# Two-layer streaming encoder trunk: head additions moved to VectorE, reload DMAs moved to GpSimd's queue, layer 0 put in another order

## The chip, the cores and the metric

One core of one Trainium2 chip runs the whole kernel. The metric is the device time of one execution in microseconds; the median of 3 runs of the kernel before is 2255.37 us (2248.55 to 2256.2). Engines: TensorE (PE; its weight loads are PEld), VectorE (DVE), ScalarE (ACT), GpSimd (POOL), SyncE (SP). A DMA is issued from the queue of SP, ACT or POOL.

## The reference

1088 frames (1024 of a new stream, 64 of a running one) of 1024 channels pass two layers:

```python
hn = rmsnorm(x, g_mix); proj = hn @ w_in           # u_a | u_b, 512 channels each
# A: 32 groups x 64 complex diagonal states
lam_bar = exp(lam * dt); b_bar = ((lam_bar - 1) / lam) * b
h[t] = lam_bar * h[t-1] + b_bar @ u_a[t]; y = Re(c @ h) + d * u_a
z = gelu(y); y_a = z * sigmoid(z @ w_glu)
# B: mean over the last 2/4/8/16 frames minus the frame, per group of 128 channels
y_b = ((window_sum / count - u_b) @ w_pool) * pool_scale
x = x + concat([y_a, y_b]) @ w_out
x = x + square(relu(rmsnorm(x, g_ffn) @ w_ff1)) @ w_ff2
```

Then a last RMSNorm. The final states and the last 15 rows of u_b are outputs too. All is float32.

## The kernel before

Channels lie on partitions, frames on the free axis: x is [128, 8, 1088]. Frames are ordered so that a block of 8 successive frames is one column of J = 136 (T = 8 * 136). A product in float32 precision is three float32r passes, high x high, low x high and high x low (`products`, L427): each weight block (512 KB in `w_raw`, two buffers) is split on ScalarE (`split_hi`, L649) and VectorE (`split_lo`, L874), and so are the activations (`h_high`/`h_low`, L879). A tile of a product is 128 x 1088 in one of two PSUM buffers; for 8 k-blocks it takes TensorE 12 us, for 4 some 6 us. `tile_done` counts tiles of TensorE, `tile_free` those that VectorE has read out. Two small PSUM buffers serve all little matmuls, in the order of `small_numbers`. Each engine's order is written out by hand; an engine does its instructions strictly in that order.

**Head.** ACT's queue loads x; ScalarE and VectorE square it by turns, GpSimd adds the squares up (`add_squares`, L1378), and h_high, h_low of all eight rows are made. `angles`, `discretised` and `rotations` on VectorE, `exponents` and `sines` on ScalarE make layer 0's tables (powers of lambda, rotations over 136 blocks by doubling: piece 0 to length 16, piece 1 to 64, pieces 2 and 3 the last step for each half).

**Window tiles (t = 0 to 7).** u_a tiles (`win_a`) go to DRAM and come back as blocks (`turn_u`); u_b tiles (`win_b`) go into `ub`, which lies in x's place. Between tiles TensorE does `turns` (transposes of the drive weights), `drives` (block inputs to states) and `kernels` (the kernel inside a block). VectorE makes `drive_weights`, `carry_weights`, `fix_kernel`, the window sums (`pooled`), and turns the states back (`pre`), scans them (`scan`) and turns them on (`post`), in quarters q = 0 to 3.

**Second half of the mixer.** Four pool tiles, `y_b` on VectorE; eight tiles `wob(n)` (half of w_out) that VectorE adds to x, which has to be loaded again first (L394, L399: SP's queue, behind `carry_weights` and eight DMAs of `intra_weights`, L390, in pieces of 512 B). `carry(q)` on TensorE makes y of quarter q from intra and carry weights; ScalarE (`carried`) empties the small buffers and stores to DRAM, SP loads `y_a` (L403, after block B_GLU + 1 has been asked for, which needs the low half of block B_WOB + 3, made in VectorE's `wob(3)`). `gelus` and z_high on ScalarE, z_low on VectorE, then the gate product, the other half of w_out, and the feed-forward part in 8 chunks (cc) of 4 up-tiles (m = 0 to 3) and 8 down-tiles. In layer 0 these chunks also hold layer 1's tables. x overlaps the pool buffers, `y_a` the states, z_high the rotations, and `kst` (stage for the intra kernel) the buffer `work_s`.

Of the kernel before, what the change touches and what calls it, by code (L numbers as in the profile page):

```python
# [9 lines left out]
ALU = mybir.AluOpType  # L10
ACT = mybir.ActivationFunctionType

P = 128
# [3 lines left out]
BLK = 8  # L17
# [4 lines left out]
KD = DM // P  # L22
# [37 lines left out]

def small_numbers():
# [16 lines left out]
    for t in range(2, 8):  # L78
        if 3 <= t < 7:
            drives(0, t - 3)  # L80
        if t < 6:
            turns(0, t - 2)
        if t >= 4:
            kernels(0, t - 4)
# [12 lines left out]
def hybrid_trunk(nc, x_in, w_blocks, w_pool, prep_in, gain0, layer_in, dstate_in,  # L97
# [10 lines left out]
    with ExitStack() as ctx:  # L108
# [50 lines left out]
        class Prep:  # L159


            def __init__(self, l):
# [15 lines left out]
                if l == 0:  # L178
                    z = E
                    self.rot_tmp = at("rot_products_0", o, [P, 2, 512])  # L180
# [56 lines left out]
        first_sq = sem("first_sq")  # L237
# [7 lines left out]
        pp_in = sem("pp_in")  # L245
        dd_in = sem("dd_in")
# [78 lines left out]
        PREP_CHUNKS = {cc: cc - 1 for cc in range(1, 5)}  # L325
# [4 lines left out]
        def _(sp):  # L330
# [28 lines left out]
            def load_prep(l):  # L359
                sp.dma_start(prep_of[l].pp[:, :], prep_in[l, :, 0:C_HIST]).then_inc(pp_in, 16)  # L360
                sp.dma_start(dd[:, :], dstate_in[l]).then_inc(dd_in, 16)

            sp.dma_start(g0[:, :], gain0).then_inc(const_in, 16)
            fetch(0)
            load_prep(0)
            fetch(1)
            for l in range(LAYERS):
                LB, LT = l * NB, l * NT
                for b in range(2, B_FF + 2):
# [12 lines left out]
                    if b == B_WOB + 2:  # L382
                        sp.wait_ge(tile_done, LT + KD)
                        sp.wait_ge(cy_out, 128 * (l + 1))
                        sp.dma_start(cy[:, :, :, :], cy_dram[l]).then_inc(cy_in, 16)
                        sp.wait_ge(k_out, 128 * (l + 1))
                        sp.wait_ge(k_zero, 32)
                        for tau in range(BLK):
                            a = CH * (BLK - 1 - tau)
                            sp.dma_start(kin[CH * tau:CH * tau + CH, :, :],  # L390
                                         k_dram[l, :, :, a:a + P]).then_inc(kin_in, 16)
                        sp.wait_ge(tile_free, LT + T_POOL + KA + 2)
                        for m in range(6):
                            sp.dma_start(x[:, m, :], (x_in, x_hist)[l][m]).then_inc(x_back[m], 16)  # L394
                    if b == B_WOB + 3:
                        sp.wait_ge(hist_out_s, 16 * (l + 1))
                        sp.wait_ge(fin_out, 16 * (l + 1))
                        for m in range(6, KD):
                            sp.dma_start(x[:, m, :], (x_in, x_hist)[l][m]).then_inc(x_back[m], 16)  # L399
# [5 lines left out]
                for b in range(B_FF + 2, NB + 2):  # L405
# [6 lines left out]
                    if l == 0 and b == B_FF + 8 * 6:  # L412
# [8 lines left out]
        def _(pe):  # L421
# [27 lines left out]
            def sum_part(phase, c):  # L449
                a, b = CHUNKS[c]  # L450
                out = small_at(SM["sum", phase, c])
                pe.wait_ge(sq_added, 7 * phase + 7)
# [48 lines left out]
            for l in range(LAYERS):  # L501
                LB, LT = l * NB, l * NT

                for t in range(KD):
# [12 lines left out]
                    if l == 0:  # L517
# [4 lines left out]
                        if t >= 4:  # L522
                            kernels(0, t - 4)
# [51 lines left out]
                if l == 0:  # L575
                    for n in range(4):
                        wob(n)
                    carry(0)
                    carry(1)
                    wob(4)  # L580
                    carry(2)
                    wob(5)
# [3 lines left out]
                else:  # L586
                    wob(0)
                    carry(0)
                    wob(1)
# [54 lines left out]
        def _(act):  # L644
# [12 lines left out]
            def finish(m, phase, gain, keep):  # L657

                if m > 2:
                    act.wait_ge(sq_added, 7 * phase + m - 2)  # L660
# [60 lines left out]
            for m in range(KD):  # L721
                act.dma_start(x[:, m, :], x_in[m]).then_inc(x_in_s[m], 16)
            split_hi(0)
            act.wait_ge(const_in, 16)
            for m in range(KD):
                act.wait_ge(x_in_s[m], 16)
                if m % 2 == 0:
                    if m > 2:
                        act.wait_ge(sq_added, m - 2)
                    act.activation((tr if m else rms)[:, :], x[:, m, :], ACT.Square).then_inc(sq_made, 1)  # L730
                act.activation(hhi[:, m, :], x[:, m, :], ACT.Copy, scale=g0[:, m:m + 1]).then_inc(hhi_made, 1)
                if m == 1:
                    exponents(0)
                if m == 3:
                    sines(0)
            split_hi(1)
            act.wait_ge(ones_set, 1)

            for l in range(LAYERS):
                LB, LT = l * NB, l * NT  # L740
                for t in range(KD):
# [3 lines left out]
                    if l == 0:  # L745
# [4 lines left out]
                        if t >= 4:  # L750
                            kernels(0, t - 4)
# [29 lines left out]
                def gelus(q):  # L781
                    act.wait_ge(ya_in[q], 16 * (l + 1))
                    act.activation(ya[:, q, :], ya[:, q, :], ACT.Gelu_apprx_tanh).then_inc(gelu_made, 1)
                    act.wait_ge(gelu_made, l * KA + q + 1)
                    if q == 0:
                        act.wait_ge(st_v, l * 4 + 4)
                    act.activation(zhi[:, q, :], ya[:, q, :], ACT.Copy).then_inc(z_made, 1)

                if l == 0:
                    wob_ahead(0)  # L790
                    wob_ahead(1)
                    carried(0)
                    carried(1)
                    carried(2)
                    wob_ahead(2)
                    carried(3)
                else:
                    carried(0)
                    wob_ahead(0)
                    carried(1)  # L800
                    wob_ahead(1)
                    carried(2)
                    carried(3)
                    wob_ahead(2)
                for q in range(4):
                    gelus(q)
# [53 lines left out]
        def _(v):  # L860
# [20 lines left out]

            def inverse(phase):
# [35 lines left out]
            def discretised(l):  # L918
# [3 lines left out]
                v.wait_ge(prep_a, l * 4 + 4)  # L922
                tt(d.th[:, :, :], d.k[:, :, :], d.k[:, :, :], ALU.mult)
# [42 lines left out]
            def doubled(l, n, h):  # L966
# [549 lines left out]
```

## Time and profile before

| | |
|---|---|
| profiled execution | 2253.69 us, span 2251.9 us, mean granted clock 0.973 |
| PE / PEld busy | 2106.2 / 2061.9 us (94% / 92%) |
| DVE / ACT / POOL busy | 1120.2 / 421.3 / 120.3 us |
| TensorE waits over the span, by releaser | h_low 36.3; x 27.5; x_quarter 12.0; y_b_low 8.8; issue (intra weights, layer 1) 7.9 |
| DMA landing, median from issue | w_raw 512 KB 3.6 us; y_a 544 KB 4.3; cy_dram 256 KB (POOL) 2.9; bt_dram 512 KB (POOL) 5.7; prep_in 736 KB 9.8 in the head |

A row of the timeline reads: start us, duration us, engine, line, operation, output<-inputs, count, and in brackets the idle time of that engine just before and what ended it. Rows of successive instructions of one kind are merged (xN). TensorE has 146 us of idle time in the span, 82 of them before 300 us.

### The profile page before, as it was taken

What the parts mean: (1) busy time and instruction counts of PE and PEld (TensorE: products, weight loads), DVE (VectorE), ACT (ScalarE), POOL (GpSimd) and SP (SyncE); (2) the same over time, 40 slices, a digit from 0 to 9 for tenths busy, and PEclk for the clock granted to TensorE, in tenths of its full rate; (3) what the DMA queues carried; (4) which work ended last, traced back from release to release, by engine and by line L of the source; (5) the groups of instructions that cost most, each with busy time, mean ns of one, the idle gap of its engine ahead of it and who ended that gap; (6) DMA issues with size and microseconds to landing.
All of it is one profiled execution on the core that took longest, in us unless ns stands there. A gap on an engine that the chain in (4) does not pass through costs nothing. (4 is left out here: it accounts for less than half of the span.)

```text
span 2251.9 us, 29009 instructions
## 1 busy us (share of the span) xinstructions
PE 2106.2 (94%) x12894; PEld 2061.9 (92%) x12894; DVE 1120.2 (50%) x1622; ACT 421.3 (19%) x483; POOL 120.3 (5%) x80
## 2 busy tenths in 40 slices
PE   4796799899999999999999989999999999999995
PEld 3785799899999999999999879999999999999995
DVE  8896646836344453434356843552433334333344
ACT  3121143201111111111131114420110111111021
POOL 4000003000000000000030000300000000000002
PEclk7898999999999999999999999999999999999997
DMA  3325521112111111311134382111111111111111
GB/s 143 103 64 96 171 58 52 47 38 96 48 57 58 54 54 49 121 48 47 38 117 133 78 174 69 38 47 48 47 38 47 47 38 47 47 47 38 48 38 79
DMA packets 72060, 152.63 MB, mean 68 GB/s; under 512 B 7392, under 2 KB 32512, under 8 KB 71296
## 3 DMA queue, kind: packets, MB, share of 16 engines
q1 hardware_dynamic: 56240, 123.25, 18.3%
q10 hardware_dynamic: 12960, 17.96, 2.5%
q0 software_dynamic: 2736, 9.57, 1.2%
q8 instruction: 101, 1.65, 0.3%
q14 instruction: 23, 0.19, 0.0%
HBM read 123.23 MB, written 27.53 MB: 67 GB/s over the span
## 5 line engine op out<-in xcount | busy, mean ns | idle before, releaser
L1214 DVE TENSOR_TENSOR x<-tile,x 128x816 f32<-128x816 f32 x320 | 216.4, 718 | 519.8 <-PE tile L427 491.7
L427 PE MATMUL tile<-h_high,w_high 128*128 128x408 f32 (+1 forms) x1920 | 432.0, 333 | 41.8 <-DVE h_low L879 36.3
L427 PE MATMUL tile<-h_low,w_high 128*128 128x408 f32 (+1 forms) x1920 | 426.0, 330 | 0.0
L427 PE MATMUL tile<-h_high,w_low 128*128 128x408 f32 (+1 forms) x1920 | 425.9, 330 | 0.0
L427 PEld LDWEIGHTS tile<-h_high,w_high 128*128 128x128 f32 x1920 | 324.0, 190 | 49.7 <-DVE h_low L879 26.7
L427 PE MATMUL tile<-hidden_high,w_high 128*128 128x408 f32 (+1 forms) x1536 | 341.6, 331 | 11.3 <-DVE x L1214 6.2
L427 PE MATMUL tile<-hidden_low,w_high 128*128 128x408 f32 (+1 forms) x1536 | 338.9, 329 | 0.0
L427 PE MATMUL tile<-hidden_high,w_low 128*128 128x408 f32 (+1 forms) x1536 | 338.8, 329 | 0.0
L649 ACT ACTIVATE w_high<-w_raw 128x1024 fp32r<-128x1024 f32 x164 | 172.4, 1051 | 824.2 <-PE tile L427 807.9
L427 PEld LDWEIGHTS tile<-h_low,w_high 128*128 128x128 f32 x1920 | 323.2, 190 | 1.2
L427 PEld LDWEIGHTS tile<-h_high,w_low 128*128 128x128 f32 x1920 | 323.1, 190 | 1.2
L1330 DVE SCALAR_TENSOR_TENSOR work_r<-tile,rms 128x816 f32<-128x816 f32 (+1 forms) x128 | 86.7, 719 | 377.6 <-PE tile L427 377.4
L427 PEld LDWEIGHTS tile<-hidden_high,w_high 128*128 128x128 f32 x1536 | 257.0, 189 | 18.1 <-issue 12.7
L874 DVE TENSOR_TENSOR w_low<-w_raw,w_high 128x1024 fp32r<-128x1024 f32 x164 | 210.4, 1283 | 101.3 <-ACT w_high L649 101.3
L427 PEld LDWEIGHTS tile<-hidden_low,w_high 128*128 128x128 f32 x1536 | 256.7, 189 | 0.9
L427 PEld LDWEIGHTS tile<-hidden_high,w_low 128*128 128x128 f32 x1536 | 256.7, 189 | 0.8
L829 ACT ACTIVATE hidden_high<-work_r 128x1088 fp32r<-128x1088 f32 x64 | 71.4, 1116 | 647.2 <-DVE work_r L1330 647.2
L1378 POOL TENSOR_TENSOR rms<-rms,work_s 128x1088 f32<-128x1088 f32 x20 | 54.6, 2732 | 1214.3 <-ACT work_s L662 1189.5
L1333 DVE TENSOR_TENSOR work_s<-work_r 128x1088 f32<-128x1088 f32 x64 | 82.7, 1292 | 2.2
L1338 DVE TENSOR_TENSOR hidden_low<-work_s,hidden_high 128x1088 fp32r<-128x1088 f32 x64 | 82.2, 1284 | 0.0
L427 PE MATMUL tile<-y_b_high,w_high 128*128 128x408 f32 (+1 forms) x192 | 44.2, 339 | 20.7 <-DVE x L1214 20.2
L879 DVE SCALAR_TENSOR_TENSOR h_low<-x,layer_params,h_high 128x1088 fp32r<-128x1088 f32 x24 | 43.9, 1830 | 27.3 <-ACT h_high L664 27.3
(156 smaller groups left out, 1445.2 us busy)
## 6 DMA issues: line engine op xcount, KB each, us to landing
w_raw<-w_blocks SPq DMA_DIRECT2D x164, 512.0 KB, 3.6
x<-x_t ACTq DMA_DIRECT2D x8, 544.0 KB, 12.4
u_blocks<-ua_dram SPq DMA_DIRECT2D x64, 68.0 KB, 2.7
x<-x_t SPq DMA_DIRECT2D x8, 544.0 KB, 13.7
ya_dram<-u_blocks ACTq DMA_DIRECT2D x64, 68.0 KB, 2.2
y_a<-ya_dram SPq DMA_DIRECT2D x8, 544.0 KB, 4.3
x_kept<-x ACTq DMA_DIRECT2D x8, 544.0 KB, 2.7
x<-x_kept SPq DMA_DIRECT2D x8, 544.0 KB, 13.0
```

The costliest lines, as they stand in the source:

```text
L427: mm = pe.matmul(ps[tile][:, c, 0:(b - a) * J], lhs, xt[:, k, a * J:b * J], start=(first and n == 0), stop=(last and n == 2))
L649: act.activation(whi[:, b % 2, :], raw[:, b % 2, :], ACT.Copy).then_inc(whi_made, 1)
L829: act.activation(ghi[:, m, :], tr[:, :], ACT.Square).then_inc(ghi_made, 1)
L874: v.tensor_tensor(wlo[:, b % 2, :], raw[:, b % 2, :], f32(whi[:, b % 2, :]), ALU.subtract).then_inc(wlo_made, 1)
L879: v.scalar_tensor_tensor(hlo[:, m, :], x[:, m, :], gain[:, m:m + 1], f32(hhi[:, m, :]), ALU.mult, ALU.subtract).then_inc(h_made, 1)
L1214: ins = v.tensor_tensor(xt, pt_, xt, ALU.add)
L1330: ins = v.scalar_tensor_tensor(out, pt_, 0.0, r, ALU.max, ALU.mult)
L1333: v.tensor_tensor(ts[:, :], tr[:, :], tr[:, :], ALU.mult).then_inc(sq_v, 1)
L1338: v.tensor_tensor(glo[:, m, :], ts[:, :], f32(ghi[:, m, :]), ALU.subtract).then_inc(hid_made, 1)
L1378: pool.tensor_tensor(rms[:, :], rms[:, :], (tr, ts)[m % 2][:, :], ALU.add).then_inc(sq_added, 1)
```

## The change

- Head: `add_first` on VectorE adds the squares (semaphore `first_added`), ScalarE squares all eight rows. `exponents(0)` and `angles(0)` go first, `sines(0)` after h_high of row 0, `discretised(0)` after the eight rows. The parameters come in two DMAs (160 KB ahead of the first weight block).
- The reloads of x, `carry_weights` and `intra_weights` go from SP's queue to POOL's, in layer 0 with six rows of x ahead of the intra weights.
- Layer 0: VectorE's rotation pieces, `pre`, `scan`, `post` and `fix_kernel` in another order; `kernels` after tiles 3, 4, 6, 7; TensorE's `wob` and `carry` in another order, in layer 1 `wob(1)` ahead of `carry(0)`.
- `gelus(0)` stands before `carried(2)`; the others alternate with z_high.
- Layer 1's tables over chunks 0 to 5 of layer 0's feed-forward part.

```diff
+KERNEL_AFTER = {3: 0, 4: 1, 6: 2, 7: 3}
-        PREP_CHUNKS = {cc: cc - 1 for cc in range(1, 5)}
+        PREP_CHUNKS = {cc: cc - 2 for cc in range(2, 6)}
# SP
             sp.dma_start(g0[:, :], gain0).then_inc(const_in, 16)
+            sp.dma_start(prep_of[0].pp[:, 0:C_BRE], prep_in[0, :, 0:C_BRE]).then_inc(pp_in, 16)
             fetch(0)
-            load_prep(0)
+            load_more(0)
             fetch(1)
-                    if b == B_WOB + 2:
-                        (carry_weights, intra_weights x8, x rows 0 to 5)
-                    if b == B_WOB + 3:
-                        (x rows 6 and 7)
# TensorE, layer 0 / layer 1
-  wob(0..3) carry(0) carry(1) wob(4) carry(2) wob(5) carry(3) wob(6) wob(7)
+  wob(0) wob(1) wob(2) carry(0) wob(3) wob(4) carry(1) wob(5) carry(2) carry(3) wob(6) wob(7)
-  wob(0) carry(0) wob(1) carry(1) wob(2) ...
+  wob(0) wob(1) carry(0) carry(1) wob(2) ...
# ScalarE, head
+            exponents(0)
             split_hi(0)
             for m in range(KD):
                 act.wait_ge(x_in_s[m], 16)
-                if m % 2 == 0:
-                    ...
                 act.activation(hhi[:, m, :], x[:, m, :], ACT.Copy, scale=g0[:, m:m + 1])
+                if m == 0:
+                    sines(0)
+                if m > 2:
+                    act.wait_ge(first_added, m - 2)
+                act.activation(((tr, ts)[m % 2] if m else rms)[:, :], x[:, m, :], ACT.Square)
# ScalarE, carries: layer 0 / layer 1
+  wob_ahead(0) carried(0) wob_ahead(1) carried(1) gelus(0) wob_ahead(2) carried(2) carried(3)
+  wob_ahead(0) carried(0) carried(1) wob_ahead(1) gelus(0) carried(2) carried(3) wob_ahead(2)
+                act.wait_ge(st_v, l * 4 + 4)
+  gelus(1) z(0) gelus(2) z(1) gelus(3) z(2) z(3)
# VectorE, head
+            def add_first(m):
+                v.wait_ge(sq_made, m + 1)
+                if m > 1:
+                    v.wait_ge(first_added, m - 1)
+                v.tensor_tensor(rms[:, :], rms[:, :], (tr, ts)[m % 2][:, :], ALU.add).then_inc(first_added, 1)
+            angles(0)
             split_lo(0)
             for m in range(KD):
                 v.wait_ge(x_in_s[m], 16)
                 low_h(m, m, g0)
+                if m > 1:
+                    add_first(m - 1)
+            add_first(KD - 1)
             split_lo(1)
+            discretised(0)
# VectorE, layer 0
+  inverse(0) win_a(0) rotations(0, 0) win_a(1) rotations(0, 1) drive_weights(0, 0) win_a(2)
+  drive_weights(0, 1) carry_weights(0, 0) win_a(3) drive_weights(0, 2) carry_weights(0, 1)
+  fix_kernel(0, 0) win_b(4) rotations(0, 2) drive_weights(0, 3) win_b(5) carry_weights(0, 2)
+  fix_kernel(0, 1) pooled(0, 3) win_b(6) carry_weights(0, 3) pooled(0, 2) fix_kernel(0, 2)
+  win_b(7) pooled(0, 1) fix_kernel(0, 3) pooled(0, 0) y_b(0..3)
+  pre(0, 0, late) scan(0, 0) wob(0) post(0, 0) wob(1) pre(0, 1, late) scan(0, 1) wob(2)
+  post(0, 1) rotations(0, 3, late) wob(3) pre(0, 2, late) wob(4) scan(0, 2) post(0, 2)
+  wob(5) pre(0, 3, late) scan(0, 3) post(0, 3) wob(6) wob(7)
# VectorE, feed-forward of layer 0: after up-tile m of chunk cc
-  cc 0: angles, discretised, rotations 0, rotations 1; cc 1, m 0: rotations 2 and 3
-  cc 1 to 4: drive_weights at m 1, carry_weights at m 3
+  cc 0: angles, discretised, rotations 0 (m 0 to 2); cc 1: rotations 1, 2, 3 (m 0 to 2)
+  cc 2 to 5: drive_weights at m 1, carry_weights at m 2
# GpSimd
-            add_squares(0)
+                carry_weights_out(0, q); kernels_out(0, q)      # q = 0 to 3
+            carry_in(0)          # waits tile_done, cy_out
+            x_first_back(0)      # waits tile_free of y_b(3), then rows 0 to 5
+            kernels_in(0)        # waits k_out, k_zero, then 8 DMAs
+            states_out(0)        # waits st_v
+            x_last_back(0)       # waits the stores, then rows 6 and 7
             add_squares(1)
             ...
+            carry_in(1); kernels_in(1); x_first_back(1); states_out(1); x_last_back(1)
```

## Rows read from the trace of the kernel before

**Rows 1.** The page, part 1: busy time and share of each engine.
```profile
PE 2106.2 (94%) x12894; PEld 2061.9 (92%) x12894; DVE 1120.2 (50%) x1622; ACT 421.3 (19%) x483; POOL 120.3 (5%) x80
```
**Rows 2.** TensorE's waits: us in total, times, longest us.
```profile
PE tile L427 <- DVE h_low L879: 36.3, 9, 12.0
```
**Rows 3.** Timeline of the head, all engines.
```profile
10.53 1.35 DVE L879 SCALAR_TENSOR_TENSOR h_low<-x,gain,h_high 128x1088 fp32r<-128x1088 f32 x1 [0.97 <-ACT h_high L731]
...
11.80 1.28 DVE L1156 TENSOR_TENSOR work_s<-x 128x1088 f32<-128x1088 f32 x1
...
47.87 3.49 POOL L1378 TENSOR_TENSOR rms<-rms,work_s 128x1088 f32<-128x1088 f32 x1 [1.28 <-DVE work_s L1156]
48.92 3.52 DVE L874 TENSOR_TENSOR w_low<-w_raw,w_high 128x1024 fp32r<-128x1024 f32 x1
...
52.58 1.25 PE L427 MATMUL tile<-h_high,w_high 128*128 128x408 f32 x3 [0.44 <-DVE w_low L874]
```
**Rows 4.** Timeline of VectorE, layer 0: rotations, reciprocals, tables, pre and scan.
```profile
52.36 0.25 DVE L987 COPY rotations<-phasor 128x16 f32<-128x16 f32 x2
...
61.38 6.97 DVE L885 RECIPROCAL rms<-rms 128x408 f32<-128x408 f32 x3
...
85.94 1.29 DVE L865 TENSOR_TENSOR rot_products<-rotations 128x512 f32<-128x512 f32 x2
...
90.27 0.69 DVE L865 TENSOR_TENSOR prep_products<-power_re,bbar_re 128x512 f32<-128x512 f32 x1
...
94.38 1.35 DVE L1174 TENSOR_TENSOR work_r<-tile,rms 128x816 f32<-128x816 f32 x2
...
231.56 2.62 DVE L865 TENSOR_TENSOR dve_products_late<-rotations,states 128x544 f32<-128x544 f32 x4
...
239.25 1.35 DVE L1214 TENSOR_TENSOR x<-tile,x 128x816 f32<-128x816 f32 x2
```
**Rows 5.** Timelines of VectorE and TensorE, last pool tile to the gate, layer 0.
```profile
201.68 1.48 DVE L1207 SCALAR_TENSOR_TENSOR y_b_low<-tile,layer_params,y_b_high 128x816 fp32r<-128x816 f32 x2 [1.51 <-ACT y_b_high L763]
...
230.29 1.35 DVE L1214 TENSOR_TENSOR x<-tile,x 128x816 f32<-128x816 f32 x2 [17.62 <-DMA x<-x_t]
...
241.64 2.63 DVE L865 TENSOR_TENSOR dve_products_late<-rotations,states 128x544 f32<-128x544 f32 x4
...
246.20 1.35 DVE L1214 TENSOR_TENSOR x<-tile,x 128x816 f32<-128x816 f32 x2
...
296.00 0.74 PE L427 MATMUL tile<-z_high,w_high 128*128 128x408 f32 x3 [2.81 <-DVE z_low L1309]
```
**Rows 6.** Timeline of VectorE: first instruction of discretised(1) and first after it.
```profile
408.04 0.44 DVE L865 TENSOR_TENSOR prep_phase<-prep_turns 128x272 f32<-128x272 f32 x1
...
414.25 1.36 DVE L1330 SCALAR_TENSOR_TENSOR work_r<-tile,rms 128x816 f32<-128x816 f32 x2
```
**Rows 7.** DMA rates: 206 to 232 us; 105.4 to 111 us, with POOL's packets.
```profile
GB/s 0 25 35 188 143 80 147 139 96 91 101 136 91 93 109 126 91 95 120 113 94 93 127 105 95 92 136 98 91 98 147 123 109 101 301 408 408 402 415 422
...
GB/s 0 0 0 0 0 0 0 0 0 0 0 146 380 293 380 293 293 88 59 351 293 322 293 322 234 0 0 0 0 0 0 0 0 0 0 0 0 0 0 59
...
q0 software_dynamic: 160, 0.52, 29.4%
```
**Rows 8.** Feed-forward, layer 0: TensorE after waits; a window with the granted clock.
```profile
444.75 1.25 PE L427 MATMUL tile<-hidden_high,w_high 128*128 128x408 f32 x3 [4.98 <-DVE x L1214]
...
521.65 1.09 PE L463 MATMUL small<-prep_in,x_quarter 128*128 128x128 f32 x8 [2.33 <-DVE x_quarter L1026]
...
447.00:450.00 3.00, 3.00 (x11) 2.94 (x11) 0.00 (x0) 0.00 (x0) 0.00 (x0) 0.50 0.60 167
```
**Rows 9.** Layer 1: TensorE at carry(0), SP's y_a loads, their landing.
```profile
1311.94 2.15 PE L564 MATMUL small<-u_blocks,intra_weights 128*128 128x136 f32 x8 [7.90 <-issue]
...
1345.74 0.91 SPq L403 DMA_DIRECT2D y_a<-ya_dram  x2
...
y_a<-ya_dram SPq DMA_DIRECT2D x8, 544.0 KB, 4.3
```

More of the change, by code:

```diff
@@ L82, in small_numbers @@
             turns(0, t - 2)
-        if t >= 4:
-            kernels(0, t - 4)
+        if t in KERNEL_AFTER:
+            kernels(0, KERNEL_AFTER[t])
     sums(1)
@@ L411, in _ @@
                         load_prep(1)
-                    if l == 0 and b == B_FF + 8 * 6:
+                    if l == 0 and b == B_FF + 8 * 6 + 3:
                         sp.wait_ge(rot_out, 16)
@@ L575, in _ @@
                 if l == 0:
-                    for n in range(4):
-                        wob(n)
+                    wob(0)
+                    wob(1)
+                    wob(2)
                     carry(0)
+                    wob(3)
+                    wob(4)
                     carry(1)
-                    wob(4)
+                    wob(5)
                     carry(2)
-                    wob(5)
                     carry(3)
@@ L587, in _ @@
                     wob(0)
+                    wob(1)
                     carry(0)
-                    wob(1)
                     carry(1)
@@ L790, in _ @@
                     wob_ahead(0)
+                    carried(0)
                     wob_ahead(1)
+                    carried(1)
+                    gelus(0)
+                    wob_ahead(2)
+                    carried(2)
+                    carried(3)
+                else:
+                    wob_ahead(0)
                     carried(0)
                     carried(1)
[L794 to L800, printed above, removed]
                     wob_ahead(1)
+                    gelus(0)
                     carried(2)
@@ L804, in _ @@
                     wob_ahead(2)
-                for q in range(4):
-                    gelus(q)
+                act.wait_ge(st_v, l * 4 + 4)
+                gelus(1)
+                z(0)
+                gelus(2)
+                z(1)
+                gelus(3)
+                z(2)
+                z(3)
                 wob_ahead(3)
@@ L980, in doubled, with rotations @@
                     tt(r[:, :, ri, :, n:2 * n], t0, t1, op)
-            def rotations(l, piece):
+            def rotations(l, piece, tmp=None):
                 d = prep_of[l]
@@ L1225, in _ @@
                     win_a(0)
+                    rotations(0, 0)
+                    win_a(1)
                     rotations(0, 1)
-                    rotations(0, 2)
-                    win_a(1)
-                    rotations(0, 3)
                     drive_weights(0, 0)
@@ L1257, in _ @@
                         y_b(i)
-                    fix_kernel(0, 3)
+                    pre(0, 0, late)
+                    scan(0, 0)
+                    wob(0)
                     post(0, 0)
+                    wob(1)
+                    pre(0, 1, late)
+                    scan(0, 1)
+                    wob(2)
                     post(0, 1)
-                    wob(0)
+                    rotations(0, 3, late)
+                    wob(3)
                     pre(0, 2, late)
+                    wob(4)
                     scan(0, 2)
-                    wob(1)
                     post(0, 2)
-                    wob(2)
+                    wob(5)
                     pre(0, 3, late)
                     scan(0, 3)
-                    wob(3)
                     post(0, 3)
-                    for m in range(4, KD):
+                    for m in range(6, KD):
                         wob(m)
```

145 lines of the change are left out of this document (68 added, 77 removed).

## The prediction

> **What bounds the kernel.** I read the shares first: TensorE is busy for 2106.2 of 2251.9 us [rows 1]. The matmuls themselves don't change, so what can be won is its 146 us of idle time and the stretches at the lower clock. The list of its waits says what ends the idle time: 36.3 us for h_low, of which most lies in the head [rows 2]. The timeline then gives the places, in this order: the head, where tile 1 starts only at 52.58 [rows 3]; the table work of layer 0 up to the transposes at 94.40 [rows 4]; the reload of x, where VectorE stood until 230.29 and TensorE 19.4 us with it [rows 5]; rotations in the feed-forward part, 4.98 us [rows 8]; and the wait for the intra weights in layer 1, 7.90 us [rows 9]. The profiled execution took 2253.7 us, 1.8 more than its span and 1.7 less than the median of 2255.4, so I sum against it and let the result stand for the median.
>
> **Head.** GpSimd's additions take 3.49 us each, and VectorE operations beside them stretch: w_low takes 3.52 there and 1.2 elsewhere [rows 3]. With the additions on VectorE each of the eight h_low (about 1.25 back to back, from 1.35 alone) is followed by an addition of 1.28 at most, so VectorE needs 2.5 us a row of x. ScalarE's two operations on a row take 2.3, so it isn't the bound. Exponents come first: the parameters (160 KB now, ahead of the weights) should be there when ScalarE has issued its x loads and its table, near 7; the angles are eight operations of 0.3 to 0.44, about 3.4 us; w_low and h_low(0) end near 13.1 (before: 11.9, so tile 0 starts 1.2 later). The sines push Square(0) to 14.2; h_low(1) ends at 16.8, and from h_low(3) on the pace is 2.5: h_low(7) ends near 31.8, the last two additions at 34.3, w_low(1) at 35.5. Tile 1 starts at 35.6 instead of 52.58. Behind it stand discretised (6.2, from its copy in layer 1 [rows 6]), and the three reciprocals (6.97, [rows 4]): 35.5 + 6.1 + 6.97 = 48.6, against 68.35. The root of the third part is needed at 46.8 and is there at 45.2. So win_a(0) comes **19.8 us earlier**. If the parameters come 4 us later, all of this does.
>
> **Window tiles.** From win_a(0) to the first transposes VectorE had 26.0 us [rows 4]. Out of it go the two last rotation pieces (4.3 each), in comes piece 0 (52.36 to 61.38, 9.0): 26.4. Transposes at 75.1 instead of 94.40, gain 19.3, and TensorE still waits some 10 us there. After that TensorE's own order sets the pace: 12.1 us a tile and 3.6 to 6.5 of small work between; kernels are moved one tile forward, the same number in all. VectorE has lost pre and scan of two quarters (7.7 each [rows 4]) there and idles 4 to 7 us before three of the tiles; these hide the rotation piece put there (4.3). ScalarE's kernels(0,0) waits for the last store of u, about 4.2 us after win_a(3), which is over before TensorE has the numbers. y_b(3) ends at 184.0 instead of 203.1 [rows 5]: gain 19.1.
>
> **Reload and carries, layer 0.** What was finished before y_b(3) now comes behind it: pre and scan of quarters 0 and 1 (15.4) and the rotation piece (4.3). Against that, x is asked for at 184.1 with no intra weights ahead of it. VectorE's chain: pre, scan to 191.7; wob(0) 193.0; post (4.56 [rows 5]) 197.6; wob(1) with its split 200; pre, scan 207.7; wob(2) 209.0; post 213.6; rotation 217.9; wob(3) 220.4; pre 224.4; wob(4) 225.7; scan 229.3; post 233.9; wob(5) 236.4; pre, scan 244.1; post 248.7. TensorE has wob(2) done at 199.4 and then needs the intra weights. They arrive late without cost up to 204.4, since wob(5) is due on VectorE at 233.9 and lies 29.5 of TensorE behind them. The order of POOL's queue is x (3.3 MB at about 410 GB/s, until 194), then the intra weights (2.1 MB). On SP's queue these moved at about 105 GB/s [rows 7], 20 us: 214. POOL's writes of carry weights, also in pieces of 512 B, moved at about 310 [rows 7], 7 us: 202. The bounds are 202 and 214, the direction being the other; I take 202, because POOL's two writes of 256 KB were 160 packets [rows 7], so that a packet holds several pieces. Then the end is VectorE's: carry(3) can't start before 248.7, TensorE has waited 12 us by then in two places and loses 2.5 to the lower clock (6 us or so of half speed follow such a gap [rows 8]); carry(3) 5.6, two tiles 12.1, one addition and z_low 2.6: the gate starts at 271.5 instead of 296.00 [rows 5]. **Gain to this point: 24.5 us.** ScalarE's gelu of quarter 0 hides there: y_a(0) is asked for after wob(3)'s split at 220.4 and ScalarE comes to it at 229. The activation table it brings forward was not what the gate waited for, so nothing for that.
>
> The Trainium skill, page "DMA: Bandwidth & Descriptors", section "Issuing engine by pattern", sends plain loads to the SP queue and calls that path generally faster, which speaks against moving them to POOL. By the two rates above, the trace says the contrary for pieces of 512 B; by the page the intra weights would be no faster than 214, which is the first rival below.
>
> **Feed-forward, layer 0.** Rotation piece 1 leaves the place just ahead of the down-projection: the wait of 4.98 goes, and with it the half-clock stretch behind it (0.50 at 447 to 450 [rows 8], some 7 us in all, 3.4 lost). The wait of 2.33 for x_quarter [rows 8] goes too, with 1.7 of clock, since the weights are made a chunk after the rotations. Pieces 1 to 3 now follow three up-tiles of 12 us on which VectorE has 5.9 of its own: 14.3, 10.2, 10.2; one overrun of 2.3 is held by the second buffer, as the 8.65 there was before. The wait of 3.9 behind piece 0 stays. **Gain 12.4**; from below 7.3, the waits alone.
>
> **Layer 1.** With wob(1) ahead of carry(0), TensorE works until 1309.9 while the intra weights land (fast 1300, slow 1311): the 7.90 and 2.2 of clock go, 10.1. But one stall comes. gelus(0) stands on ScalarE before carried(2), and y_a(0) is only asked for when SP has fetched past wob(3)'s split (before: 1345.74, right behind it [rows 9]). wob(3) now ends at 1333.2, the split at 1335.8; the load lands about 4.3 later [rows 9], with a weight block beside it some 1341; gelu to 1342. TensorE's carry(2) has filled both small buffers at 1335.5 and waits for ScalarE to empty one: 6.5 us, and 2.5 of clock. Net gain **1.1**; 10.1 if the stall is not there, and a loss of 2 if the load takes 7.
>
> **Sum.** 24.5 + 12.4 + 1.1 = 38.0; 2253.7 - 38.0 = 2215.7, say **2216 us**.
>
> **Rivals.**
> A. The intra weights move no faster on POOL's queue. They land at 214: 9.6 us beyond the slack, 2.5 of clock for the gap of 14.6, 1.4 in layer 1. 2216 + 13.5 = 2229. For: both SP transfers of this kind show 105. Against: POOL's packets.
> B. No stall at gelus(0) in layer 1, because the y_a load is quick or the gap too short to lower the clock: 2207 to 2212. For: some y_a loads in layer 0 took less than the median. Against: the order on SP fixes the request at 1336.
> C. The head gives less: VectorE's chain with the sines on ScalarE starts late (the parameters had 9.8 us to land before, for 736 KB) or the small steps cost more in their places: 5 to 8 us less, 2222.
> D. Slower than before: POOL's loads don't overlap but run one after another, at the 2.9 us that a write of 256 KB took and 5.7 for 512 KB. 6 x 5.7 + 8 x 2.9 = 57 us puts the intra weights at 241 and the gate at 306, 10 us later than before; layer 1 loses some 12 by x behind the intra weights; 12.4 come back in the feed-forward part: about 2263. It decides from intra weights later than 245 alone, or 230 with layer 1 hit too. Against: two POOL writes, issued one right behind the other, moved 512 KB in under 5 us with a gap of one slice or two [rows 7].
> E. The change doesn't do what it says: VectorE, now with more behind y_b(3), was the bound all along, and the earlier head is given back there beyond what I counted. 2240 to 2256; against it stand the 17.62 us in which VectorE waited for x [rows 5].
>
> **Chances.** The forecast 0.50 (2211 to 2221), A 0.18, B 0.12, C 0.12, D 0.03, E 0.05. Faster by over 0.5% (11 us, about what a measurement can tell from no change) is all but D and a part of E: 0.94; within 0.5%: 0.03; slower: 0.03. The range reaches from B to a little beyond A: 2205 to 2232.
>
> **What would show it.** Tile 1 at 35 to 37 and the reciprocals' end near 49; transposes near 75; y_b(3) near 184; no wait of VectorE for x; intra weights at about 300 GB/s and landed near 202; a TensorE gap of some 9 us ahead of carry(3), released by VectorE; the gate near 271. The up-part of chunk 0 without the 4.98. In layer 1 a gap of 6 or 7 us inside carry(2), released by ScalarE. The forecast is wrong if h_low keeps a pace above 2.5, if the intra weights are later than 204, or if another engine's order holds a quarter that I took as free.

## The result

Seven runs of each kernel: 2241.92 us against 2255.37, ratio 0.9942 (95% interval 0.9928 to 0.9957). The forecast was 2216 with a range from 2205 to 2232. The change gains 13.4 us where 39 were expected, and the time lies outside the range.

The profiled execution took 2241.92 us, its span is 2240.1. The engines' busy time and share, against [rows 1]:

```profile
PE 2103.8 (94%) x12894; PEld 2058.9 (92%) x12894; DVE 1109.3 (50%) x1625; ACT 424.9 (19%) x487; POOL 116.9 (5%) x107
```

TensorE's waits (us in total, times, longest). h_low has fallen from 36.3 [rows 2], but three carry waits together make 45.9:

```profile
PE tile L419 <- DVE h_low L882: 22.2, 9, 13.7
PE small L559 <- issue: 21.6, 2, 18.1
PE small L559 <- ACT u_blocks L769: 13.4, 9, 7.0
PE small L458 <- DVE x_quarter L1036: 11.6, 1, 11.6
PE small L559 <- DVE states L1151: 10.9, 1, 10.9
```

The timeline of the head and the tables, answering [rows 3, 4]. Tile 1 starts at 36.31 instead of 52.58, the reciprocals end near 49.3 instead of 68.4, the transposes start at 75.69 instead of 94.40:

```profile
34.95 1.22 DVE L877 TENSOR_TENSOR w_low<-w_raw,w_high 128x1024 fp32r<-128x1024 f32 x1
36.31 1.25 PE L419 MATMUL tile<-h_high,w_high 128*128 128x408 f32 x3 [2.07 <-DVE w_low L877]
42.29 6.98 DVE L894 RECIPROCAL rms<-rms 128x408 f32<-128x408 f32 x3
...
75.69 1.97 PE L458 MATMUL small<-prep_in,x_quarter 128*128 128x128 f32 x8 [11.60 <-DVE x_quarter L1036]
```

From y_b(3) to the gate, answering [rows 5]. The wait for x (17.62) is gone, and the first add to x comes at 194.14 instead of 230.29. Then TensorE stands 18.14 us before carry(0):

```profile
184.97 1.48 DVE L1213 SCALAR_TENSOR_TENSOR y_b_low<-tile,layer_params,y_b_high 128x816 fp32r<-128x816 f32 x2 [2.80 <-ACT y_b_high L758]
186.75 3.20 POOL L1407 DMA_DIRECT2D x<-x_t  x6 [15.21 <-DVE y_b_low L1213]
189.94 5.02 POOL L1421 DMA_DIRECT2D intra_weights<-k_dram  x8
194.14 1.33 DVE L1220 TENSOR_TENSOR x<-tile,x 128x816 f32<-128x816 f32 x2
...
219.94 2.15 PE L559 MATMUL small<-u_blocks,intra_weights 128*128 128x136 f32 x8 [18.14 <-issue]
...
233.23 1.35 DVE L1220 TENSOR_TENSOR x<-tile,x 128x816 f32<-128x816 f32 x2 [12.97 <-PE tile L419]
...
250.24 1.36 DVE L1220 TENSOR_TENSOR x<-tile,x 128x816 f32<-128x816 f32 x2 [1.14 <-PE tile L419]
...
253.14 1.23 DVE L877 TENSOR_TENSOR w_low<-w_raw,w_high 128x1024 fp32r<-128x1024 f32 x1 [1.55 <-ACT w_high L646]
...
266.67 2.18 PE L559 MATMUL small<-u_blocks,intra_weights 128*128 128x136 f32 x8 [10.90 <-DVE states L1151]
...
290.44 0.73 PE L419 MATMUL tile<-z_high,w_high 128*128 128x408 f32 x3 [2.81 <-DVE z_low L1318]
```

"issue" there names no releaser. The DMA rates between 165 and 205 us, one number a us, do: x moves at about 410 (396 to 422) from 190 until about 197.5, then the intra weights at 102 to 115. It is the rate of [rows 7], on the other queue:

```profile
GB/s 216 324 57 0 0 8 66 262 229 360 426 524 262 33 0 0 0 0 0 0 0 0 0 226 279 422 405 421 396 413 418 422 173 107 111 102 102 107 115 107
```

Three windows (length, PE busy, granted clock, busy share of the sixteen DMA engines, GB/s). The DMA engines count as fully busy with x at 414 GB/s and with the intra weights at 118. In the third, the stretch before and at carry(3), TensorE had stood 10.90 us, and the clock granted is 0.50, the level of 1.2 GHz:

```profile
190.00:197.00 7.00, 6.98 (x43) 1.00 1.02 414
200.00:216.00 16.00, 1.80 (x12) 0.72 1.04 118
260.00:275.00 15.00, 7.85 (x44) 0.50 0.40 127
```

Layer 1, answering [rows 9]. The wait before carry(0) is 3.47 instead of 7.90; a new one of 7.01 stands inside carry(2), and the matmuls behind it take 2.18 instead of 1.19:

```profile
1195.35 1.15 PE L490 MATMUL small<-u_blocks,drive_weights 128*64 128x136 f32 x16 [0.36 <-ACT states L703]
...
1295.92 2.15 PE L559 MATMUL small<-u_blocks,intra_weights 128*128 128x136 f32 x8 [3.47 <-issue]
...
1331.04 2.18 PE L559 MATMUL small<-u_blocks,intra_weights 128*128 128x136 f32 x8 [7.01 <-ACT u_blocks L769]
...
1367.89 1.25 PE L419 MATMUL tile<-z_high,w_high 128*128 128x408 f32 x3 [2.81 <-DVE z_low L1318]
```

The same three places before the change were 296.00, 1213.60 (a run of drives early in layer 1) and 1379.50 (its gate). So the change stands 5.6 us ahead at layer 0's gate, 18.3 ahead at layer 1's drives and 11.6 ahead at its gate. In sum: layer 0 gains 5.6, the feed-forward part 12.7, layer 1 loses 6.6.

### The profile page after: what moved, and what is told of

Its sections match the earlier page's. It is cut to its first block and busy times, and to the rows that moved or that the text cites. A ratio compares the mean times of both kernels' runs of the same rounds, so it can differ in the third digit from the quotient of the medians.

```text
span 2240.1 us, 29012 instructions
## 1 busy us (share of the span) xinstructions
PE 2103.8 (94%) x12894; PEld 2058.9 (92%) x12894; DVE 1109.3 (50%) x1625; ACT 424.9 (19%) x487; POOL 116.9 (5%) x107
## 5 line engine op out<-in xcount | busy, mean ns | idle before, releaser
L1380 POOL TENSOR_TENSOR rms<-rms,work_s 128x1088 f32<-128x1088 f32 x16 | 40.7, 2541 | 1082.1 <-ACT work_s L659 1082.1
L559 PE MATMUL small<-u_blocks,intra_weights 128*128 128x136 f32 x128 | 23.5, 338 | 45.9 <-issue 21.6
L559 PEld LDWEIGHTS small<-u_blocks,intra_weights 128*128 128x128 f32 x128 | 20.3, 233 | 48.5 <-issue 22.9
```

Source lines behind the costliest of these rows:

```text
L559: pe.matmul(sm[gl][:, i * J:(i + 1) * J], kin[:, 2 * (u + i) + gl, :], ublk[:, 2 * (u + i) + gl, :], start=(i == 0), stop=False)
L1380: pool.tensor_tensor(rms[:, :], rms[:, :], (tr, ts)[m % 2][:, :], ALU.add).then_inc(sq_added, 1)
```

## The experiments

Theory after the result: the intra weights behind x take 20 us at 105 GB/s, and this uses up what the head gained; in layer 1, gelus(0) in front of carried(2) costs TensorE 7 us and some of its clock. Rival: VectorE's chain behind y_b(3) was the bound anyway (rival E of the prediction). In the comparisons below the kernel before stood at 2254.5 to 2255.7 us.

**Which term is which.** `e1_intra_first` puts the intra weights ahead of x:

```
             carry_in(0)
+            kernels_in(0)
             x_first_back(0)
-            kernels_in(0)
```

> The changed kernel with one edit: in layer 0 GpSimd's queue loads the intra weights ahead of the six rows of x (as SP did before, and as layer 1 still does). Theory (the gain of the head is lost to intra weights that move at about 105 GB/s on this queue too, 21 us of it behind x, so that carry(0) starts at 219.9 instead of 204): the intra weights land near 195, x row 0 near 197, 3 us later than VectorE asks for it; carry(0) no longer waits, VectorE's chain sets the gate at about 277 instead of 290.4, the time falls by 13 to about 2229. Rival (VectorE's chain with pre and scan of quarters 0 and 1 behind y_b was the bound anyway): the gate stays at 288 to 291 and the time at 2240 to 2242. Second rival (TensorE at half clock): carry(3) keeps its 8.9 us and wins nothing.

Measured 2234.16, ratio 0.991 (0.9893 to 0.9926): 7.8 us better than the change. The wait for the intra weights is gone and a smaller one for x has come. In VectorE's and TensorE's timelines:

```profile
200.28 1.35 DVE L1220 TENSOR_TENSOR x<-tile,x 128x816 f32<-128x816 f32 x2 [8.79 <-DMA x<-x_t]
201.78 1.24 PE L419 MATMUL tile<-y_b_high,w_high 128*128 128x408 f32 x3 [8.20 <-DVE x L1220]
212.15 1.19 PE L559 MATMUL small<-u_blocks,intra_weights 128*128 128x136 f32 x8 [0.48 <-ACT u_blocks L769]
...
257.07 2.18 PE L559 MATMUL small<-u_blocks,intra_weights 128*128 128x136 f32 x8 [7.72 <-DVE states L1151]
...
279.83 0.73 PE L419 MATMUL tile<-z_high,w_high 128*128 128x408 f32 x3 [2.81 <-DVE z_low L1318]
```

VectorE's chain alone didn't hold the gate in the change: with another order of the same loads it came at 279.83 instead of 290.44. In the change VectorE took 72.5 us from its first addition to x to the start of carry(3) (194.14 to 266.67). Of these it waited 15.7: 12.97 and 1.14 for tiles of TensorE, which had stood for the intra weights, and 1.55 for ScalarE. In e1 the same way takes 56.8 us (200.28 to 257.07) without such waits; the forecast had 57.0. So a late load holds the chain, and once both loads are there the chain sets carry(3). The size lay between the two expectations: x came at 200.28, not at 197, and carry(3) took 7.9 us at the lower clock against 8.9 in the change, so a part of the second rival holds. One of the two loads is late in either order.

`e2_gelu_late` (layer 1, ScalarE):

```
                     wob_ahead(1)
-                    gelus(0)
                     carried(2)
                     carried(3)
+                    gelus(0)
```

> The changed kernel with one edit: in layer 1 gelus(0) stands behind carried(3) on ScalarE. Theory (ScalarE waits for y_a of quarter 0 with TensorE's full small buffers behind it, 7.0 us, then half clock): the stall inside carry(2) goes, the time falls by 8 to 9, to about 2233. Rival (the stall only stands in for a later one, since the gate waits for z_low anyway): under 3 us, 2239 or more.

Measured 2229.98, ratio 0.9892 (0.9878 to 0.9907): 11.9 us better. The 7.01 is gone. Carry(0) and the gate of layer 1 in this profile:

```profile
1291.22 1.59 PE L559 MATMUL small<-u_blocks,intra_weights 128*128 128x136 f32 x8 [2.69 <-issue]
...
1354.01 1.25 PE L419 MATMUL tile<-z_high,w_high 128*128 128x408 f32 x3 [2.81 <-DVE z_low L1318]
```

From carry(0) to the gate layer 1 takes 62.8 us instead of 72.0, so 9.2 belong to the edit: 6.5 of stall (7.01 where 0.48 stands otherwise) and some 2.6 of clock, as the prediction had it (6.5 and 2.5). In this profile the drives of layer 1 also came 3.9 us earlier, on unchanged code: in layer 0 carry(0) started at 216.99 instead of 219.94, and between 260 and 275 us the granted clock was 0.74 instead of 0.50. The runs of the change itself spread over 8.6 us, so I credit the edit with 9, not 12.

`e3_both` has the two edits together.

> Both edits of the two runs before. If the two causes are separate the gains add: 21 to 22 us, about 2220, which is within 5 of the 2216 that was predicted. If they share a bound: 2228 or more.

Measured 2222.70, ratio 0.9857 (0.9843 to 0.9872). Together the edits gain 19.2, against 7.8 and 11.9 alone and 21 to 22 expected: within the intervals the parts add up. On top of e1_intra_first the gelu edit gains 11.5 us by the times, but 9.0 between carry(0) and the gate of layer 1 (73.2 to 64.2). The other 2 to 3 us lie outside this stretch, here as in e2_gelu_late, and no run shows their cause.

**The parts of the change, alone.** `f1_tables_alone` is the kernel before with nothing but layer 1's tables over six chunks:

```
-        PREP_CHUNKS = {cc: cc - 1 for cc in range(1, 5)}
+        PREP_CHUNKS = {cc: cc - 2 for cc in range(2, 6)}
...
+                            if cc == 0 and m < 3:
+                                (angles, discretised, lambda l: rotations(l, 0))[m](1)
+                            elif cc == 1 and m < 3:
+                                rotations(1, 1 + m)
```

> The kernel before with one part of the change: layer 1's tables over chunks 0 to 5 of the feed-forward part. Theory (predicted 12.4, and 12.7 between the traces): about 2242, nearly the whole net effect of the change. Rival (the part lives on something else in the change): under 6 us.

Measured 2242.85, ratio 0.995 (0.9933 to 0.9966), as expected. This part alone gives 11.6 of the 13.4 us. The change as it stood is 0.9 us faster than this one part (2241.92 against 2242.85), which is less than the intervals: all the other parts together gave nothing that the times can show.

`h1_head_gpsimd` is the changed kernel with the head's additions given back to GpSimd:

```
# VectorE
-                if m > 1:
-                    add_first(m - 1)
-            add_first(KD - 1)
# GpSimd
+            for m in range(1, KD):
+                ...
+                pool.tensor_tensor(rms[:, :], rms[:, :], (tr, ts)[m % 2][:, :], ALU.add).then_inc(first_added, 1)
```

> The changed kernel with one part undone: GpSimd adds the squares in the head again, VectorE does not; all else in the head stays. Theory (GpSimd's additions at 3.5 us each set the pace and stretch VectorE's operations beside them): seven additions from 17.6 to 42, w_low(1) some 8 us later than 34.9, and everything behind it, up to the end, 7 to 9 us later: about 2250. Rival (the head's gain is lost on the way to the gate, where the intra weights set the time): no change, since these too start later only by what VectorE is later, so this rival says under 3 us, 2245 or less.

Measured 2246.26, ratio 0.9967 (0.9955 to 0.9979), 4.3 us worse than the change. That is between the two expectations (7 to 9, and under 3). The timelines, head and carry(0):

```profile
27.81 3.38 POOL L1442 TENSOR_TENSOR rms<-rms,work_r 128x1088 f32<-128x1088 f32 x1
...
42.98 0.85 PE L419 MATMUL tile<-h_high,w_high 128*128 128x408 f32 x3 [1.79 <-DVE w_low L877]
...
82.73 1.97 PE L458 MATMUL small<-prep_in,x_quarter 128*128 128x128 f32 x8 [11.57 <-DVE x_quarter L1036]
...
225.44 2.15 PE L559 MATMUL small<-u_blocks,intra_weights 128*128 128x136 f32 x8 [18.04 <-issue]
```

Tile 1 is 6.7 us later than in the change and the transposes are 7.0, so this one edit makes about a third of the head's 19.1. The rest should come from exponents, Squares and the order of the tables, but none of these was undone alone. TensorE is 5.1 us later at the gate (295.55): most of what the head gives does reach the gate, so the rival is out. It also corrects the theory above: the late load doesn't use up the head's gain, it costs its own share beside it.

**Why the intra weights move at 105 GB/s.** `e4_two_queues` is e3_both with half of their DMAs on SP's queue:

```
-                for tau in range(BLK):
+                for tau in range(BLK // 2):
...
+                        for tau in range(BLK // 2, BLK):
+                            a = CH * (BLK - 1 - tau)
+                            sp.dma_start(kin[CH * tau:CH * tau + CH, :, :],
+                                         k_dram[l, :, :, a:a + P]).then_inc(kin_sp, 16)
```

> Both edits, and the eight DMAs of the intra weights split over two queues in both layers: four on GpSimd's, four on SP's, at the same time. Theory P (a DMA of this kind is slow because it writes 16 partitions only, so two at once on different partitions go twice as fast): about 210 GB/s, landed some 10 us after the start instead of 20; x row 0 is no longer late in layer 0 (3 us) and the wait of 3.5 in layer 1 goes: about 2214. Theory E (the sixteen DMA engines are the bound at one 512 B piece each 78 ns, whatever the queue): 105 GB/s together, same time as with both edits alone, 2220.

Measured 2219.15, ratio 0.9841 (0.9826 to 0.9855), 3.6 us better than e3_both. A window of the load, e3_both first, then e4_two_queues:

```profile
180.00:195.00 15.00, 15.00 (x80) 0.89 1.04 116
180.00:195.00 15.00, 15.00 (x81) 0.90 1.16 120
```

The two queues together are hardly faster than one, so neither the queue nor the issuing engine is the limit. The weights land 1 us earlier in layer 0 and some 2 in layer 1, and there that is enough to end the wait before carry(0), 2.23 us in e3_both.

Two kernels then changed the shape of the load. In `d1_long_pieces` the intra weights are read 16 KB in a row, into the same 16 partitions a DMA; in `d2_all_partitions` each DMA brings pieces of 512 B to all 128 partitions, read from the carry weights. In both, mixer output y is computed with intra weights that hold other data.

```
# d1
+                    pool.dma_start(kin[CH * tau:CH * tau + CH, :, :].rearrange("p g n -> p (g n)"),
+                                   k_dram[l].rearrange("c g n -> c (g n)")[:, 0:GROUPS * P]).then_inc(kin_in, 16)
# d2
+                    h = 4 * (tau // 2)
+                    pool.dma_start(kin[:, 4 * tau:4 * tau + 4, :],
+                                   cy_dram[l, :, h:h + 4, tau % 2, :]).then_inc(kin_in, 16)
```

> Intra weights first and gelu late (as in e3_both), but each of the eight intra-weight DMAs reads 16 KB in a row for each of its 16 partitions (the first 4096 numbers of a row of the stage in DRAM, so the y of mixer A is not the reference's); same bytes, same 16 partitions, same queue. If the pieces of 512 B are the cause of 105 GB/s: 300 to 400 GB/s here, landed 6 us after the start, x row 0 in time in layer 0, no wait ahead of carry(0) in layer 1, about 2213. If the 16 partitions are: 105 GB/s and 2222.

> The same, but each of the eight DMAs reads 512 B pieces, four for each of all 128 partitions, from the stage of the carry weights (y of mixer A is not the reference's). If the pieces are the cause: 105 GB/s again. If the 16 partitions are: 300 or more, the written piece of 512 B being no hindrance in the carry weights' stores either.

Measured 2212.6 (ratio 0.9813, 0.9788 to 0.9838) and 2209.39 (one run). The times alone don't decide: d1's is the one expected if the pieces are the cause, d2's goes with the partitions. The rates tell them apart; 165 to 205 us, of e3_both, e4_two_queues, d1_long_pieces and d2_all_partitions in this order:

```profile
GB/s 228 246 180 0 0 8 62 184 246 377 410 377 459 242 86 115 127 98 127 98 102 107 127 123 107 135 98 131 115 136 110 151 338 396 418 405 418 413 409 300
```

```profile
GB/s 136 0 0 0 0 8 57 238 180 344 410 394 437 291 92 104 148 104 126 128 110 148 94 130 134 94 135 97 124 122 120 304 413 396 408 413 416 413 413 409
```

```profile
GB/s 242 217 0 0 8 53 209 147 410 475 344 459 311 197 115 164 147 115 147 115 180 115 164 115 197 58 116 165 360 405 400 414 413 418 418 218 57 0 0 25
```

```profile
GB/s 230 274 0 0 8 33 180 115 393 360 459 393 340 332 295 295 283 295 291 176 121 257 400 409 413 430 400 409 409 113 17 0 0 0 0 29 131 340 25 0
```

In each row the carry weights come first (to 475), then the intra weights, then x (about 410). e3's 17 slices that begin with 86 and end with 110 have a mean of 114, e4's 16 from 92 to 120 of 118. Pieces 32 times as long, into 16 partitions, give 134 (the 13 slices of d1 that begin with 115 and end with 116); the same short pieces into 128 partitions give about 290. What holds the rate is first the number of partitions in a DMA, and only then the length of the pieces: the pieces alone are ruled out. One thing stays open. Every slow load also reads from 16 rows of `k_dram`, and d2 reads from 128 rows of another tensor, at other starting addresses. No run varied the reading side alone, so that it is the writing of 16 partitions is argued, not shown.

The Trainium skill, page "SBUF — State Buffer", section "Door 1: The DMA port swizzle (why `[64,N]` ≈ `[32,N]`)", has this rule: a transfer's rate goes with the SBUF ports that its partitions reach, partitions 0 to 15 reach four of sixteen, and its table gives 104 GB/s for them. The traces agree for pieces of 512 B: 105 on SP's queue [rows 7], about 107 on POOL's in the change and 114 in e3_both, 118 with the second queue. The 134 of d1_long_pieces lies above the 104, and above the 109 that the table has as the limit for these partitions: there the measurement counts, and the rule is right only roughly. It would have made rival A the forecast.

**A version that uses it.** `e8_shifted` makes the eight shifted copies when the kernels are written (VectorE's and ScalarE's work is the same), so that the reload is one transfer of 128 partitions by 16 KB (the writes of zeros and TensorE's new index aren't shown):

```
-    k_dram = nc.dram_tensor("k_dram", (LAYERS, CH, GROUPS, 240), F32, kind="Internal").ap()
+    k_dram = nc.dram_tensor("k_dram", (LAYERS, P, GROUPS, P), F32, kind="Internal").ap()
...
+                for tau in range(BLK):
+                    pool.dma_start(k_dram[l, CH * tau:CH * tau + CH, 8 * q:8 * q + 8, CH * tau:P],
+                                   prep_of[l].kst[:, :, :, 0:P - CH * tau].rearrange("p a g n -> p (a g) n")
+                                   ).then_inc(k_out, 16)
...
+                pool.dma_start(kin[:, :, :], k_dram[l]).then_inc(kin_in, 16)
```

> As e3_both, but the intra weights' eight shifted copies are made when the kernels are written: each quarter's k_stage goes out in eight transfers (was two), shifted by 16 tau, and the zeros of both layers go out behind the first two quarters, so that the reload is one transfer of 128 partitions x 16 KB, as the carry weights' is. Two earlier looks, at kernels whose intra weights held other data, said: 16 KB pieces into 16 partitions at a time about 150 GB/s, 512 B pieces into all 128 partitions about 290 GB/s, against 105 for 512 B into 16. Theory (the few partitions, and then the short pieces, hold the rate): the load moves at the carry weights' 300 to 400 GB/s, 2.1 MB in under 7 us, x follows 12 us earlier, the wait for x is gone, layer 1 likewise, and the time is that of those two looks, 2209 (2206 to 2213). Rival 1 (reading DRAM that was written a few us before is what is slow): the rate stays near 105 and the time near e3's 2222.7. Rival 2 (the 24 more issues, 0.5 us each on GpSimd's queue, hold the last quarter or the k_stage buffer): the rate is high, but the weights leave later and a TensorE or ScalarE wait for k_stage appears, 2213 to 2218.

Measured 2209.01 (2208.62 to 2209.83), ratio 0.9795 (0.9781 to 0.9808): 46.7 us faster than before and 32.9 than the change. Of the latter 19.2 are the two edits of e3_both, 13.7 the shape of the load. The rates of the same 40 us, with carry and intra weights together at up to 492 GB/s and both landed by 185, and POOL, ScalarE and TensorE in the timeline:

```profile
GB/s 378 359 176 1 12 119 90 58 25 213 279 311 459 459 377 475 459 360 492 279 33 52 261 383 361 282 339 409 418 418 344 100 0 0 0 0 0 111 360 53
```

```profile
166.82 0.59 ACT L696 ACTIVATE k_stage<-small 16x512 f32<-16x512 f32 x1 [5.78 <-DMA k_dram<-k_stage]
...
168.90 4.18 POOL L1401 DMA_DIRECT2D k_dram<-k_stage  x8 [3.72 <-DVE k_stage L1076]
173.08 0.59 POOL L1420 DMA_DIRECT2D carry_weights<-cy_dram  x1
174.58 0.57 POOL L1426 DMA_DIRECT2D intra_weights<-k_dram  x1 [0.91 <-DMA k_dram<-k_stage]
...
203.11 1.19 PE L559 MATMUL small<-u_blocks,intra_weights 128*128 128x136 f32 x8 [0.48 <-ACT u_blocks L769]
...
234.88 2.18 PE L559 MATMUL small<-u_blocks,intra_weights 128*128 128x136 f32 x8 [6.33 <-DVE states L1151]
...
249.65 2.18 PE L559 MATMUL small<-u_blocks,intra_weights 128*128 128x136 f32 x8 [7.67 <-DVE states L1151]
...
271.41 0.74 PE L419 MATMUL tile<-z_high,w_high 128*128 128x408 f32 x3 [2.81 <-DVE z_low L1318]
```

The gate comes at 271.41, and TensorE waits 14.0 us for VectorE in two places. The prediction had 271.5 and 12. Rival 1 of this run (memory just written reads slowly) is out. Of rival 2 a part came true: ScalarE waits 5.78 us for the writes of an earlier quarter before it may fill k_stage again, and POOL 0.91. But the last quarter's eight issues end at 173.08, the load lands in time, and TensorE has no wait for either, so it costs nothing here.

**Other orders.** `e5_intra_parts` asks for three quarters of the intra weights behind tile 7, then the fourth, x, and the carry weights last; `e6_scan_early` is e3_both with pre and scan of quarter 0 ahead of win_b(5) on VectorE; `e7_parts_scan` has both.

```
# e5
+                if q == 3:
+                    kernels_in(0, slice(0, 24))
                 kernels_out(0, q)
-            carry_in(0)
+            kernels_in(0, slice(24, GROUPS))
             x_first_back(0)
-            kernels_in(0)
+            carry_in(0)
# e6
                     drive_weights(0, 3)
+                    pre(0, 0)
+                    scan(0, 0)
                     win_b(5)
```

> The changed kernel with gelus(0) late in layer 1 and, in layer 0, another order of loads on GpSimd's queue: intra weights of quarters 0 to 2 as soon as tile 7 is done, those of quarter 3 when they are stored, then six rows of x, carry weights last. The same 105 GB/s, but 15 of the 20 us now lie ahead of the last kernel. Theory: x row 0 lands near 190, ahead of VectorE's need at 194; carry weights near 202, carry(0) no later than that; the gate at 275 instead of 280.6 with both edits, the time 2217. Rival (VectorE's chain alone counts and x row 0 was not late by more than 3): 2220 or more.

> Both edits as in e3_both, and pre and scan of quarter 0 (7.7 us of VectorE) moved back ahead of tile 5's read-out, where VectorE idles 7 us. Theory (x row 0, landing at 200, now starts VectorE's chain): no gain, 2221 to 2223. Rival (the length of VectorE's chain behind y_b alone sets the gate): 6 to 8 us less, 2215.

> Both moves: loads in parts and pre and scan of quarter 0 early. Theory: x row 0 at 190 lets the shorter chain count, 3 to 5 us under e5_intra_parts: about 2213. Rival (carry weights or intra weights now hold carry(0) and all behind it): the same as e5_intra_parts.

Measured 2217.55 (0.9834, 0.9817 to 0.985), 2222.54 (0.9859, 0.9844 to 0.9874) and 2218.01 (0.9839, 0.9825 to 0.9854). e5's time came as expected; in its profile the gate stands at 271.41 (expected 275) and carry(0) of layer 1 still waits 4.83 us for the load. e6 gives nothing, as its theory had it. For e7 I expected 2213, and it is no better than e5: in e7's profile TensorE waits 4.18 us for the carry weights, which now land last, and 10.38 for VectorE before carry(3). The earlier scan doesn't shorten the latter because VectorE then stands for x:

```profile
194.45 1.36 DVE L1220 TENSOR_TENSOR x<-tile,x 128x816 f32<-128x816 f32 x2 [9.03 <-DMA x<-x_t]
```

In e5 this addition starts at 191.93 without a wait. In e7 GpSimd asks for x at 188.97 instead of 186.45, since the writes of the last kernel quarter, which it waits for, land 2.5 us later. From the addition to carry(3) it takes 59.0 us, 57.4 in e5, and 56.8 in e1_intra_first, e3_both, e6 and e8_shifted: once the loads are there this chain is what counts, and it begins with x.

## Why the prediction was wrong

- **Head: right.** Tile 1 at 36.31 (35.6), the reciprocals' end at 49.3 (48.6), transposes at 75.69 (75.1).
- **Window tiles: right within 2.4 us.** y_b(3) ended at 186.4, not 184.0. The gain was 18.7 at the transposes, 18.0 at pool tile 2 (174.42 for 192.42) and 16.7 at y_b(3): pool tiles 2 and 3 ran at half clock before as well, but now for longer, and VectorE's last wait for y_b_high is 2.80 instead of 1.51.
- **Reload: the step that failed.** "The bounds are 202 and 214 [...] I take 202, because POOL's two writes of 256 KB were 160 packets". The argument went by the queue and the packets, and the rate belongs to neither. Those writes read all 128 partitions of y_quarter; they say nothing on a load into 16 partitions. carry(0) started at 219.94, 15.5 beyond the slack, and the gate came at 290.44 instead of 271.5: 18.9 lost. By the timeline 2.4 of these come from y_b(3), 15.5 arise between VectorE's first addition to x and carry(3), where it waited 15.7, and 1.0 behind carry(3). The rest of the step was sound: VectorE's chain of 57.0 us measured 56.8 in four runs, and in e8_shifted, where the load is fast, the gate stands at 271.41. That the last agrees to 0.1 is in part luck, since there the weights land ahead of x, carry(3) starts 1.0 later than forecast and the end takes 1.0 less, and e5_intra_parts reaches the same 271.41 with the slow load begun earlier.
- **Rival A had the mechanism and was priced too low**, 13.5 us. Its 214 lacked the later y_b(3) and the first byte's way: 3.3 MB of x ended at 198, not 194, and the intra weights took some 21 us.
- **The order of two loads** wasn't weighed. With the intra weights at 105 GB/s TensorE's wait for x (19.36, [rows 5] has VectorE's 17.62) only becomes a wait for them (18.14). That alone would leave the gain of the head as it was. But pre, scan and a rotation piece stand behind y_b(3) now, and TensorE waits 10.90 more before carry(3). The forecast had such waits too (12 in two places), but not those for the load: from y_b(3) to the gate it takes 104.1 us, where it took 92.9 before and 87.5 were forecast. So 16.7 us at y_b(3) arrive at the gate as 5.6.
- **Feed-forward: right**, 12.7 for 12.4; alone 11.6 to 12.5 us (f1_tables_alone, against 2254.5 and 2255.4).
- **Layer 1: the stall was right, the sum not.** The wait inside carry(2) was 7.01, 6.5 more than the 0.48 that stands there otherwise, as predicted. But carry(0) still waits 3.47 for the same slow load, and carry(0) and (1) back to back wait 2.10 for ScalarE to empty the small buffers, which I left out; the clock fell twice. Layer 1 lost 6.6 where 1.1 was to be gained.
- By these terms: 2216 + 18.9 (gate) + 7.7 (layer 1) - 0.3 = 2242.3, measured 2241.9.

## What to carry over

Read a DMA's rate together with how many partitions it covers, before its queue or the length of its pieces; if a trace has one slow load, the same shape on another queue is the same load. When a wait is removed by moving a load ahead of another one, price the one that is now behind with its own measured rate, and sum up to the next point where both are needed. A stall on TensorE cost here its length and some 40% more at the lower clock (6.5 and 2.6 us).

## What was not expected of the hardware

- DMAs of 256 KB in pieces of 512 B moved at 107 to 114 GB/s into 16 partitions (from 16 rows) and at about 290 into 128 (from 128 rows); 16 KB pieces into 16 partitions at 134. The sixteen DMA engines counted as fully busy at 118 GB/s (share 1.04) as at 414 (1.02).
- Two DMA queues with the same slow load shared one rate: 92 to 148 GB/s a slice together in e4_two_queues (mean 118), 86 to 136 in e3_both (mean 114).
- 48 more DMAs on GpSimd's queue in e8_shifted (64 kernel writes instead of 16) took 0.52 us each there. ScalarE waited 5.78 us for such writes once, GpSimd 0.91, TensorE not at all.
- In e7_parts_scan and e5_intra_parts two writes of 32 KB that were asked for while the slow load was running landed late: GpSimd waited 13.51 and 11.56 us for them, and 1.05 in e3_both, where the load comes behind them.
